# Decay sums of a state-space scan: one fp32 product against two rounded products of a split factor

## What is computed

```python
def step(state, inp):
    xc, ac, bc, cc = inp
    acum = jnp.cumsum(ac.astype(jnp.float32), axis=1)
    seg = acum[:, :, None] - acum[:, None, :]
    decay = jnp.exp(jnp.where(causal, seg, -jnp.inf))
    cb = jnp.einsum('blgn,bsgn->blsg', cc, bc).astype(jnp.float32)
    y_diag = jnp.einsum('blsgr,bsgrp->blgrp', cb[..., None] * decay, xc)
    y_off = jnp.einsum('blgn,bgrpn->blgrp', cc, state) * jnp.exp(acum)[..., None]
    to_end = jnp.exp(acum[:, -1:] - acum)
    new_state = (state * jnp.exp(acum[:, -1])[..., None, None]
                 + jnp.einsum('blgn,blgr,blgrp->bgrpn', bc, to_end, xc))
    return new_state, y_diag + y_off
```

## Time and profile before

| | us |
|---|---|
| median of 3 runs (4790.35 to 4792.45) | 4792.39 |
| the profiled execution | 4796.61 |
| its span, first to last instruction | 4794.6 |
| TensorE busy in it | 4500.8 (94%) |
| VectorE busy in it | 2516.5 (52%) |
| GpSimd busy in it | 351.0 (7%) |
| decay sums on TensorE, 2180 to 2605 (64 records, two for each fp32 product) | 41.2 |
| `spread` on GpSimd, 2135 to 2598 (32 instructions) | 41.3 |

### The profile page before, as it was taken

How to read it: one execution, slowest core, us unless ns; L and a number is a source line. 1 busy time by engine, 2 the same in 40 slices (tenths; PEclk the granted TensorE clock), 3 DMA queues, 4 the chain that set the end, 5 groups by cost and what they waited for, 6 DMA issues and landing times. The chain is left out here.

```text
span 4794.6 us, 58495 instructions
## 1 busy us (share of the span) xinstructions
PE 4500.8 (94%) x21966; PEld 3752.4 (78%) x21966; DVE 2516.5 (52%) x3583; ACT 1451.7 (30%) x1547; POOL 351.0 (7%) x218
## 2 busy tenths in 40 slices
PE   8999989999999799988886998899999999999997
PEld 7887668888887588878885797677778888888886
DVE  4333444333335643347777233458887885455554
ACT  3222443222223432233333112233333333222222
POOL 0000000000000000001221000000000000333331
PEclk9999999999998999999997999899999999999998
DMA  3232112232321132221111232155554656655553
GB/s 115 97 90 77 40 40 92 98 91 97 102 87 45 24 95 99 88 74 53 52 53 32 70 96 88 64 155 136 134 141 139 202 178 208 210 193 193 193 192 106
DMA packets 514507, 519.84 MB, mean 108 GB/s; under 512 B 41173, under 2 KB 475469, under 8 KB 513374
## 3 DMA queue, kind: packets, MB, share of 16 engines
q1 hardware_dynamic: 514398, 518.41, 35.1%
HBM read 444.94 MB, written 73.40 MB: 108 GB/s over the span
## 5 line engine op out<-in xcount | busy, mean ns | idle before, releaser
L78 DVE TENSOR_TENSOR w_lo<-w_raw,w_hi 128x2048 fp32r<-128x2048 f32 (+2 forms) x326 | 674.8, 2071 | 924.5 <-ACT w_hi L72 924.3
L72 ACT CAST w_hi<-w_raw 128x2048 fp32r<-128x2048 f32 (+2 forms) x326 | 557.4, 1713 | 1292.6 <-PE psum L3072 491.6
L94 PE MATMUL psum<-h_hi,w_hi 128*128 128x512 f32 x1544 | 612.4, 397 | 33.5 <-DVE sw_q_t L1418 18.3
L95 PE MATMUL psum<-h_lo,w_hi 128*128 128x512 f32 x1544 | 606.8, 393 | 0.0
L96 PE MATMUL psum<-h_hi,w_lo 128*128 128x512 f32 x1544 | 606.2, 393 | 0.0
L94 PE MATMUL psum<-h_hi_peer,w_hi 128*128 128x512 f32 x1104 | 437.7, 397 | 23.6 <-DVE w_lo L2919 15.9
L96 PE MATMUL psum<-h_hi_peer,w_lo 128*128 128x512 f32 x1104 | 431.3, 391 | 0.0
L95 PE MATMUL psum<-h_lo_peer,w_hi 128*128 128x512 f32 x1104 | 430.8, 390 | 0.0
L3070 PE MATMUL psum<-pr_act_hi,w_hi 128*128 128x512 f32 x1024 | 398.3, 389 | 0.0
L3072 PE MATMUL psum<-pr_act_hi,w_lo 128*128 128x512 f32 x1024 | 398.3, 389 | 0.0
L3071 PE MATMUL psum<-pr_act_lo,w_hi 128*128 128x512 f32 x1024 | 398.3, 389 | 0.0
(11 more groups left out here) (464 smaller groups left out, 7582.0 us busy)
## 6 DMA issues: line engine op xcount, KB each, us to landing
w_raw<-in_ffn_w_gate_up_dram SPq DMA_DIRECT2D x176, 512.0 KB, 4.1
w_raw<-in_peer_u_dram SPq DMA_DIRECT2D x256, 256.0 KB, 4.6
w_raw<-in_peer_v_dram SPq DMA_DIRECT2D x128, 512.0 KB, 4.3
w_raw<-in_w_in_dram SPq DMA_DIRECT2D x64, 512.0 KB, 4.3
peer_hidden<-pr_q SPq DMA_DIRECT2D x64, 512.0 KB, 4.1
peer_gates<-pr_staged SPq DMA_DIRECT2D x8, 4096.0 KB, 12.9
pr_back<-peer_hidden SPq DMA_DIRECT2D x64, 512.0 KB, 6.2
pr_gate<-peer_gates SPq DMA_DIRECT2D x64, 512.0 KB, 7.1
```

Of the source, the lines that this page charges most:

```text
L72: c.nc.scalar.copy(c.hi[:, slot, :cols], c.raw[:, slot, :cols]).then_inc(c.hi_ready, 1)
L78: c.nc.vector.tensor_tensor(c.lo[:, slot, :cols], c.raw[:, slot, :cols], c.hi[:, slot, :cols].bitcast(F32), ALU.subtract).then_inc(c.lo_re ...
L94: c.nc.tensor.matmul(out, w_hi, x_hi, start=(n == 0), stop=False)
L95: c.nc.tensor.matmul(out, w_hi, x_lo, start=False, stop=False)
```

## The change

The fp32 product of the decay sums becomes two products of rounded operands (fp32r) that add up in the same PSUM bank. `adt` is split once, in the setup, into a rounded part and a rounded rest (`adt_parts`); the stationary ones matrix gets an fp32r copy (`unit`). These are three more VectorE steps ahead of `dt_end`, for which GpSimd's start waits. GpSimd then lays out both parts: each `spread_dt` issues two multiplications, one for each part, into a pair of buffers. TensorE waits for both.

```diff
-DT_STEPS = 12
+DT_STEPS = 15
...
-        spread = sb("spread", [P, 2, G_HEADS, P])
+        spread = [sb(f"spread_{n}", [P, 2, G_HEADS, P], F32R) for n in ("hi", "lo")]
+        adt_parts = [sb(f"adt_{n}", [P, TC + 1, DT_HEADS], F32R) for n in ("hi", "lo")]
+        unit = sb("unit", [P, P], F32R)
...
-                pool.tensor_tensor(spread[:, t % 2], c.tri_up[:, :].unsqueeze(1).broadcast_to([P, G_HEADS, P]),
-                                   wide(of_group(dec.adt[:, t, :], i), P), ALU.mult).then_inc(spread_done, 1)
+                for part, adt in zip(spread, adt_parts):
+                    pool.tensor_tensor(part[:, t % 2], c.tri_up[:, :].unsqueeze(1).broadcast_to([P, G_HEADS, P]),
+                                       wide(of_group(adt[:, t, :].bitcast(F32), i), P), ALU.mult
+                                       ).then_inc(spread_done, 1)
...
+            step(V.tensor_copy(unit[:, :], c.ones[:, :]))
+            step(V.tensor_copy(adt_parts[0][:, :, :], dec.adt[:, :, :]))
+            step(V.tensor_tensor(adt_parts[1][:, :, :], dec.adt[:, :, :], adt_parts[0][:, :, :].bitcast(F32),
+                                 ALU.subtract))
...
-                pe.wait_ge(spread_done, i * TC + t + 1)
+                pe.wait_ge(spread_done, (i * TC + t) * 2 + 2)
...
-                nc.tensor.matmul(sums_ps, c.ones[:, :], spread[:, t % 2].rearrange("p r l -> p (r l)"), start=True,
-                                 stop=True).then_inc(sums_ready, 1)
+                for n, part in enumerate(spread):
+                    mm = nc.tensor.matmul(sums_ps, unit[:, :], part[:, t % 2].rearrange("p r l -> p (r l)"),
+                                          start=(n == 0), stop=(n == 1))
+                mm.then_inc(sums_ready, 1)
```

## The result

The changed kernel takes 4820.84 us in the median of six runs (4816.99 to 4828.67), the kernel before 4792.42. The ratio is 1.0063, with a 95% interval of 1.0050 to 1.0076: slower by 28 us. The profiled execution took 4819.62 us with a span of 4817.9.

A forecast was written before the change was run, and what follows sets the result against it. The prediction saw each group as a loop of two stretches bound by VectorE, which GpSimd's layouts shut out; 10.2 + 9.8 + 2.8 = 22.8 us on 4792.4 gave 4815, own range 4808 to 4820, wider range 4796 to 4833.

The forecast's parts named there:

- Stretch B: Inside a group, chunk 0's sums through VectorE to chunk 1's second half and `channels(3)`: 1.27 us longer, 10.2 in eight groups.
- E: Measured piece of the group loop, not forecast: VectorE's line 1917 of chunk 0 to the second half of chunk 1.
- D: Measured piece of the group loop, not forecast: meta product to VectorE's line 1917 of chunk 0, that is, the sums.
- rival 1: TensorE's clock falls also in the second halves and `channels(3)` of 7 groups: 9.8 us more, 4825; chance 0.33.
- the walk: Group 2's VectorE and GpSimd instructions retimed, each waiting for the other's whole instruction: 1.27 us longer, 0.85 saving included.
- Stretch A: Between groups, VectorE from `rstd` to the second convolution, ScalarE's copy, `channels(2)`: 1.40 us longer in 7 places, 9.8.
- The open point: Whether the fourth layout holds VectorE's three-operand convolution step (line 1906): bounds 0 and 1.04 us, 0.6 taken.
- The clock: TensorE's longer wait before `channels(2)` lowers its clock in two more products: 2 x 1.4 = 2.8 us (0 to 2.8).
- C: Measured piece of the group loop, not forecast: `channels(2)` to the meta product, TensorE's products, transposes and wait for `meta_in`.
- Costs of nothing: Three setup steps (1.0 us), covered by VectorE's and GpSimd's idle time, and group 0's two extra `spread`: no cost.
- Rival 2: GpSimd's extra instructions fit in VectorE's gaps, only chunk 0's saving (6.8 us) is left: 4786; chance with half case 0.14.
- Rival 3: TensorE sets the pace and all four chunks' shorter sums count: 16.4 us saved, 4776; chance 0.08.

The follow-up runs named there:

- the single layout: The changed kernel with one GpSimd layout in place of two, the rounded part laid out once and multiplied twice: 4796.48 us, ratio to before 1.0007.
- the wait filled: The changed kernel with sixteen unread 128x512 products in TensorE's wait before `channels(2)`, groups 1 to 6: 4807.06 us, ratio to before 1.0032.
- the best kernel here: The kernel before with all single fp32 layouts placed in VectorE's gaps, chunk 3's in the last group after chunk 1's `skip`: 4768.72 us, 0.53% faster.

## Why the prediction was right, step by step

**The sum.** 22.8 us were forecast; the profiled executions differ by 23.0 (4819.62 against 4796.61). The median came out 5.8 above the 4815 forecast, just over the forecast's own range of 4808 to 4820 and inside the wider one up to 4833: the profiled execution of before stood 4.2 above its median and that of after 1.2 below. A difference of two profiled executions is no better than the spread of the runs. And that the profiled sum fits to 0.2 us is luck in part: the forecast had A 1.2 too large, the clock 2.6 and B 0.6 too small, and outside the three terms 1.6 us were gained.

**Stretch B** was right in size and working: +10.8 (E +17.2, D -6.4), forecast 10.2. About 1.6 of it is TensorE's clock (rival 1 below), which the walk had at nothing; without it B is 9.2. The walk through group 2 put the ends of `x_dt`, `cb` and line 1928 at 2.33, 3.38 and 4.42 us after the start of line 1917; group 3 above shows 2.35, 3.39 and 4.41. The `x_end` in line, which the walk added, is there. Of the 0.85 a group for shorter sums, 0.8 came. It was no gain by itself, as the single layout shows; the walk was right because it took the start and the collisions together.

**Stretch A** was right in mechanism and a little too large: +8.6, forecast 9.8. The end of the fourth layout came 7.20 us after `rstd`'s multiplication, as worked out. The open point is settled: line 1906's step is held. From the start of `rstd`'s multiplication its end moved by 1.33 us, forecast 1.40, and `channels(2)` by 1.21 to 1.23 in the places between groups 1 and 5. The last 0.1 is a wait of VectorE inside the next convolution, ahead of its second three-operand step: 0.26 us in the kernel before, 0.15 now. The first place grew by 0.95 alone, since that wait had been 0.54 there.

**The clock** was mis-sized: +5.4, forecast 2.8, with 2.8 as its upper bound. That the two stretches still at full clock would fall was right. The bound was not: it took the 8.10 us of the earlier trace rows as the price of a low stretch, but those windows had a granted clock of 0.79, partly recovered. In two groups of after the first 8.10 us read 0.62 and 0.61, and the whole of C lasted 10.96 and 10.99 us, against 9.72 to 9.76 where they read 0.79 and 8.2 at 1.00. With the wait filled C fell by 11.5, more than the change had added, since the kernel before had paid for this wait too.

**Costs of nothing** held. The rounded layout takes 1.03 to 1.04 us where nothing is in its way, as the fp32 one; the loop starts no later.

**The rivals.** Rival 1 happened, at a quarter of its price. The wait before the second half of chunk 0 grew by 1.8 us a group in the mean, not by the 0.8 that the rival started from, and that half took 1.94 us in six groups, all but groups 0 and 3; in group 1:

```profile
2248.84 1.94 PE L2116 MATMUL psum<-ssd_x_dt,ssd_seg 128*128 128x64 f32 x8 [2.73 <-POOL ssd_x_end L1759]
```

From there to the second half of chunk 1 it was 5.44 to 5.65 us in these groups instead of 5.23, 1.6 us in all, and in groups 2 and 5 that second half took 0.5 us longer as well: some 2.5 us against 9.8 forecast, because `channels(3)` was back at the full level. Rival 2 fell with every held instruction above. Its half case was put at 4792 +/- 5; by the prediction's own terms B's cost without A's is 10.2, so 4803, a slip that decided nothing. Rival 3 fell with the single layout: with the sums of all four chunks shorter, nothing was gained.

**What the prediction did not see** is the size of what the kernel before already paid. It named the collisions in the earlier trace rows and priced only those that were added. Placing the single layout removes the old ones and the low clock behind them: 11 us in A, 6 in C, 8 in E and 2 in D, 27 us of the profiled loop. By the medians the best kernel here beats it by 24.

## What to carry to other kernels

Before giving a nearly idle GpSimd more work, lay its timeline beside VectorE's and walk both with the rule that, where both read SBUF as these do, one waits for the other's whole instruction: the walk came out to a few hundredths of a microsecond here, while busy shares (8% and 53%) said nothing. What the waits do to TensorE's clock was the term that the walk could not give. Then ask where VectorE waits or reads PSUM, and move GpSimd's work there with a wait on VectorE's progress and one more buffer; that was worth 24 us here, where the shorter products were worth none. A step made shorter just ahead of a collision saved nothing here, and with the collisions moved it still saved nothing, in part because TensorE's clock fell.

## What the runs showed of the hardware

- A memset on GpSimd, which reads nothing, held a tensor_scalar of VectorE until 0.28 us after its end in all 8 groups, and never a tensor_tensor with two SBUF inputs (`cb` 0.28 us in all 8 groups, the multiplication by `rstd` 2.06 with and without it).
- VectorE's three-operand step with two SBUF inputs is held like tensor_tensor: up to 1.43 us instead of 0.77.
- More work made TensorE faster: 96 extra products took 14 us off the time; the granted clock after the wait was 1.00 instead of 0.61 to 0.79.
- Dropping three unused tiles and laying one scratch tile over another, with no instruction added or moved, made what follows the state-space loop 4.7 us longer: TensorE's products on the tiles `mix_y` and `mix_s` then start 231 to 238 ns apart instead of 226 to 227, at a granted clock of 1.00.
